# Reordering the attention part of the two "b1" phases: banks, weights, gates and convolution taps of a two-block network on one core

## The reference

```python
def hybrid_layer(x, ...):
    h = rmsnorm(x, norm_g)
    proj = h @ w_in                          # 1024 -> 3584
    y_a = conformer_conv(a_u, a_v, ...) * silu(a_z)   # 31-tap depthwise conv, layernorm, silu
    y_b = short_gated_conv(b_b, b_c, b_x, ...) * silu(b_z)
    y_c = window_gqa(c_q, c_k, c_v, sink) * silu(c_z)         # 4 query heads, 2 kv heads, rope
    y_d = neighborhood_attn(d_q, d_k, d_v, rpb) * silu(d_z)   # 4 heads, bias and mask
    return x + concatenate([y_a, y_b, y_c, y_d]) @ w_out
```

## Time and profile before

| | |
|---|---|
| median of three runs | 1233.93 us (1233.7 to 1235.58) |
| profiled execution | 1233.93 us, its span 1231.9 us |
| PE | busy 1222.0 us, 99% |
| DVE | busy 868.5 us, 71% |
| ACT | busy 682.1 us, 55% |
| POOL | busy 159.1 us, 13% |
| first b1 phase on PE | about 7 to 121 us |
| second b1 phase on PE | about 121 to 235 us |

### The profile page before, as it was taken

How to read it: one execution, slowest core, us unless ns; L and a number is a source line. 1 busy time by engine, 2 the same in 40 slices (tenths; PEclk the granted TensorE clock), 3 DMA queues, 4 the chain that set the end, 5 groups by cost and what they waited for, 6 DMA issues and landing times.

```text
span 1231.9 us, 24119 instructions
## 1 busy us (share of the span) xinstructions
PE 1222.0 (99%) x10072; PEld 1152.8 (94%) x10072; DVE 868.5 (71%) x1368; ACT 682.1 (55%) x1102; POOL 159.1 (13%) x210
## 2 busy tenths in 40 slices
PE   9999999999999999999999999999999999999997
PEld 7889888999999988899999999999998889999997
DVE  6998799877675567777676556667546777766742
ACT  7565665755554475565555445455447556555541
POOL 4102500473001200021000100000120003000001
PEclk9999999999999999999999999999999999999999
DMA  8545644556555554336555556555555434565551
GB/s 315 193 145 175 227 137 155 189 189 221 186 189 196 185 171 138 128 135 219 188 183 194 190 184 208 189 204 195 191 164 187 135 124 138 206 206 191 187 188 35
DMA packets 61387, 221.08 MB, mean 179 GB/s; under 512 B 7264, under 2 KB 7392, under 8 KB 61024
## 3 DMA queue, kind: packets, MB, share of 16 engines
q1 hardware_dynamic: 60768, 218.87, 53.2%
q0 software_dynamic: 224, 0.53, 0.2%
q10 hardware_dynamic: 288, 0.16, 0.0%
HBM read 218.48 MB, written 1.05 MB: 178 GB/s over the span
## 4 chain that ended last, share of the span: by engine, by line
PE 93%; DVE 3%; POOL 1%; DMA 1%; issue 1%; ACT 0%; SPq 0%; POOLq 0%; DVEq 0%; ACTq 0%
PE pb L486 13%; PE pb L484 13%; PE pb L485 13%; PE pb L499 8%; PE pb L501 8%; PE pb L500 8%; PE pb L464 7%; PE pb L466 7%; PE pb L465 7%; PE pb L559 3%; PE pb L588 1%; DVE s_acc L1367 1%; DVE s_wl L1225 1%; PE pb L616 1%; DMA s_wraw<-in_w 1%
## 5 line engine op out<-in xcount | busy, mean ns | idle before, releaser
L1225 DVE TENSOR_TENSOR s_wl<-s_wraw,s_wh 128x1024 fp32r<-128x1024 f32 (+1 forms) x411 | 503.9, 1247 | 120.0 <-ACT s_wh L868 119.6
L868 ACT ACTIVATE s_wh<-s_wraw 128x1024 fp32r<-128x1024 f32 (+1 forms) x411 | 420.4, 1049 | 183.2 <-PE pb L486 83.0
L484 PE MATMUL pb<-s_xh,s_wh 128*128 128x256 f32 x1296 | 359.1, 277 | 0.0
L486 PE MATMUL pb<-s_xh,s_wl 128*128 128x256 f32 x1296 | 358.3, 276 | 0.0
L485 PE MATMUL pb<-s_xl,s_wh 128*128 128x256 f32 x1296 | 358.3, 276 | 0.0
L485 PEld LDWEIGHTS pb<-s_xl,s_wh 128*128 128x128 f32 x1296 | 243.5, 188 | 0.0
L484 PEld LDWEIGHTS pb<-s_xh,s_wh 128*128 128x128 f32 x1296 | 243.5, 188 | 0.0
L486 PEld LDWEIGHTS pb<-s_xh,s_wl 128*128 128x128 f32 x1296 | 243.4, 188 | 0.0
L499 PE MATMUL pb<-s_hh,s_wh 128*128 128x256 f32 x660 | 182.2, 276 | 0.0
L500 PE MATMUL pb<-s_hl,s_wh 128*128 128x256 f32 x660 | 182.2, 276 | 0.0
L501 PE MATMUL pb<-s_hh,s_wl 128*128 128x256 f32 x660 | 182.2, 276 | 0.0
(11 more groups left out here) (316 smaller groups left out, 1566.8 us busy)
## 6 DMA issues: line engine op xcount, KB each, us to landing
s_wraw<-in_w SPq DMA_DIRECT2D x407, 512.0 KB, 4.0
s_nab<-in_rpb SPq DMA_DIRECT2D x2, 1024.0 KB, 8.9
s_x<-in_x SPq DMA_DIRECT2D x4, 256.0 KB, 6.0
out_dram<-s_at_s SPq DMA_DIRECT2D x4, 256.0 KB, 2.7
s_cst<-in_cst SPq DMA_DIRECT2D x1, 680.0 KB, 10.1
s_wraw<-in_w SPq DMA_DIRECT2D x2, 256.0 KB, 4.4
s_ln<-in_lng POOLq DMA_DIRECT2D x2, 128.0 KB, 7.3
s_ln<-in_lnb POOLq DMA_DIRECT2D x2, 128.0 KB, 7.9
```

The lines of the kernel that those rows point to most:

```text
L484: pe.matmul(o, wh[:, s, w], xk[0], start=k == v == 0, stop=False, skip_group_check=True)
L486: r = pe.matmul(o, wl[:, s, w], xk[0], start=False, stop=k == 7, skip_group_check=True)
L868: return act.activation(o, src, ACT.Copy, scale=scale)
L1225: dve.tensor_tensor(wl[:, s, part], wraw[:, r, part], wh[:, s, part].bitcast(F32), ALU.subtract).then_inc(low_done, 1)
```

## The change

It touches only the two b1 phases. On PE: the transposes of C's queries and keys come at tile 22 (first layer) or 23 (second), not at 26. The transposes of C's second half of weights come at tile 39, not 42. `weigh` for C and for the first half of D moves from tile 46 to tile 42, and only the second half of D stays at 46, where the transposes of the gates now follow it. The names `yC`, `yD`, `zC`, `zD` change places in the bank order. On ACT: silu of `az` is taken straight from PSUM between the exponentials of the two halves, where it was a copy there and a silu later; C's second exponentials come one unit later. On DVE: `low_c(1)` moves behind two weight units and four taps; `low_d(1)`, the products with the gates and the last taps move too, and two small steps of the lower bounds are in another place. `zc` has its own memory in place of that of `cr1`, and the turned weights of D's two halves share two slots, so ACT waits for `weighed_d0` before it copies the second.

```diff
@@ MISC["b1"], end of the tuple
-           ... "tC10", "tC11", "tD10", "tD11", "zC", "zD", "yC", "yD", "conv", "bx", "yA", "bz"),
+           ... "tC10", "tC11", "tD10", "tD11", "yC", "yD", "zC", "zD", "conv", "bx", "yA", "bz"),
@@ memory
+    zc = sb("zc", [P, 512], F32, arena)
-    zc = cr1[:, :, :].rearrange("p t c -> p (t c)")[:, 0:512]
-    at1 = Attention(arena, "at1", 8)
+    at1 = Attention(arena, "at1", 6)
@@ turned_slot
         if a == "D":
-            return 6 * t + kt
+            return kt
@@ PE, mixers1
-            tiles(n, 26)
+            tiles(n, 23 if l else 22)
             pe.wait_ge(rope_done, 2 * l + 2)
             turn_block(n, "cq", ...)
             turn_block(n, "ck", ...)
+            tiles(n, 26)
...
             tiles(n, 36)
             turn_weights(n, "D", 0)
             score_d(1)
+            tiles(n, 39)
+            turn_weights(n, "C", 1)
             tiles(n, 42)
-            turn_weights(n, "C", 1)
             turn_weights(n, "D", 1)
+            weigh(n, "C", value_c)
+            pe.wait_ge(dv_done, 2 * l + 2)
+            weigh(n, "D", value_d, (0,), (weighed_d0, 1))
             tiles(n, 46)
+            weigh(n, "D", value_d, (1,))
             for j, a in enumerate("CD"):
                 pe.wait_ge(gate_done[a], 2 * l + 2)
                 turn_block(n, "z" + a, ...)
-            weigh(n, "C", value_c)
-            pe.wait_ge(dv_done, 2 * l + 2)
-            weigh(n, "D", value_d)
@@ ACT, mixers1
+            split(n, 16)
+            act.wait_ge(*full(n, "cq"))
+            copy(flat(cqt[:, :, :]), psum(n, "cq")[:, :]).then_inc(*empty(n, "cq"))
             split(n, 17)
...
             turned_weights(n, "C", 0, 1, None)
-            exponential(n, "C", 1)
             for t in range(2):
                 act.wait_ge(main_done, projected(n, 3, t))
                 copy(dv[:, t, :], ...).then_inc(dv_done, 1)
-                copy(az[:, t, :], ..., r(t)).then_inc(*empty(n, ("in", 3, t)))
+            for t in range(2):
+                act.activation(az[:, t, :], psum(n, ("in", 3, t))[:, 256:512], ACT.Silu, scale=r(t)).then_inc(
+                    *empty(n, ("in", 3, t)))
             split(n, 22)
+            exponential(n, "C", 1)
+            split(n, 23)
             turned_weights(n, "D", 0, 0, None)
             turned_weights(n, "D", 0, 1, None)
+            split(n, 24)
             exponential(n, "D", 1)
+            turned_weights(n, "C", 1, 0, None)
+            turned_weights(n, "C", 1, 1, None)
             split(n, 25)
...
-            turned_weights(n, "C", 1, 0, None)
-            turned_weights(n, "C", 1, 1, None)
+            act.wait_ge(weighed_d0, l + 1)
             turned_weights(n, "D", 1, 0, None)
             turned_weights(n, "D", 1, 1, None)
-            act.activation(az[:, :, :], az[:, :, :], ACT.Silu).then_inc(az_done, 1)
@@ DVE, mixers1
             split(n, 19)
-            low_c(1, "tC01")
             conv(16 if l else 13)
             split(n, 20)
             conv(17 if l else 14)
...
             split(n, 21)
             conv(19 if l else 16)
+            low_c(1, "tC01")
+            split(n, 22)
+            conv(21 if l else 17)
+            split(n, 23)
             low_d(1, "tD01")
...
+            if l:
+                conv(25)
+                split(n, 25)
+                gated("C", 0)
+                gated("D", 1)
+                conv(28)
             split(n, 26)
             conv(29 if l else 26)
-            split(n, 27)
-            conv(31 if l else 27)
             product("C", zc)
             product("D", zd)
-            conv(31 if l else 28)
+            conv(30 if l else 27)
             product_low("C", zc, 4)
             product_low("D", zd, 6)
+            split(n, 27)
             conv(31 if l else 29)
```

More of the change, by code:

```diff
@@ L126 @@
     "b1": ("sum", "gate", "cq", "ck", "dq", "dk", "sC0a", "sC0b", "sD0a", "sD0b", "tC00", "tC01", "sC1a", "sC1b",
-           "tD00", "tD01", "sD1a", "sD1b", "tC10", "tC11", "tD10", "tD11", "zC", "zD", "yC", "yD", "conv", "bx", "yA", "bz"),
+           "tD00", "tD01", "sD1a", "sD1b", "tC10", "tC11", "tD10", "tD11", "yC", "yD", "zC", "zD", "conv", "bx", "yA", "bz"),
     "f": ("sum", "rbc"),
@@ L340, in program @@
     ya_done, cv_done, dv_done, rope_done = sem("ya_done"), sem("cv_done"), sem("dv_done"), sem("rope_done")
-    yh_done, az_done = sem("yh_done"), sem("az_done")
+    yh_done, weighed_d0 = sem("yh_done"), sem("weighed_d0")
     gate_done = {a: sem("gate_done" + a) for a in "CD"}
@@ L603, in turn_weights, with weigh @@
                     turn(o[:, P * h:P * (h + 1)], s[:, h, P * kt:P * (kt + 1)], fill(n, name) if h == 3 else None)
-        def weigh(n, a, value, ts=(0, 1)):
+        def weigh(n, a, value, ts=(0, 1), done=None):
             kts = [keys_of(a, t) // P for t in range(2)]
@@ L618, in weigh @@
                                           skip_group_check=True)
-            r.then_inc(*fill(n, "y" + a))
+            r.then_inc(*(done or fill(n, "y" + a)))
         def turn_block(n, name, src, count=2):
@@ L986, in mixers1 @@
             split(n, 18)
-            act.wait_ge(*full(n, "cq"))
-            copy(flat(cqt[:, :, :]), psum(n, "cq")[:, :]).then_inc(*empty(n, "cq"))
             act.wait_ge(*full(n, "dq"))
@@ L1002, in mixers1 @@
                 copy(dv[:, t, :], psum(n, ("in", 3, t))[:, 0:256], r(t)).then_inc(dv_done, 1)
-                copy(az[:, t, :], psum(n, ("in", 3, t))[:, 256:512], r(t)).then_inc(*empty(n, ("in", 3, t)))
+            for t in range(2):
+                act.activation(az[:, t, :], psum(n, ("in", 3, t))[:, 256:512], ACT.Silu, scale=r(t)).then_inc(
+                    *empty(n, ("in", 3, t)))
             split(n, 22)
+            exponential(n, "C", 1)
+            split(n, 23)
             turned_weights(n, "D", 0, 0, None)
             turned_weights(n, "D", 0, 1, None)
+            split(n, 24)
             exponential(n, "D", 1)
+            turned_weights(n, "C", 1, 0, None)
+            turned_weights(n, "C", 1, 1, None)
             split(n, 25)
@@ L1016, in mixers1 @@
                     *empty(n, ("in", 4, t)))
-            turned_weights(n, "C", 1, 0, None)
-            turned_weights(n, "C", 1, 1, None)
+            act.wait_ge(weighed_d0, l + 1)
             turned_weights(n, "D", 1, 0, None)
             turned_weights(n, "D", 1, 1, None)
-            for t in range(2):
-                act.wait_ge(*gone(n, ("in", 3, t)))
-            act.activation(az[:, :, :], az[:, :, :], ACT.Silu).then_inc(az_done, 1)
             split(n, 26)
@@ L1310, in lower_bounds_start @@
             lb = [pcols("lb", 4 * j, 4) for j in range(2)]
-            m, e0, e1 = (lbt[:, j, :] for j in range(3))
+            m, e0, e1, s = (lbt[:, j, :] for j in range(4))
             dve.wait_ge(ld_par, 16)
@@ L1316, in lower_bounds_start @@
             dve.tensor_tensor(e1, lb[1], m, ALU.subtract).then_inc(lb_step, 1)
+            dve.wait_ge(lb_exp, 2)
+            dve.tensor_tensor(s, e0, e1, ALU.add).then_inc(lb_step, 1)
+            dve.wait_ge(lb_step, 4)
+            dve.reciprocal(s, s).then_inc(lb_step, 1)
         def lower_bounds_end():
@@ L1321, in lower_bounds_end @@
             top = float(np.float32(1.0 - 1e-6))
[L1322 to L1325, removed]
             dve.wait_ge(lb_step, 5)
@@ L1459, in conv_gate @@
                 dve.wait_ge(act_a_done, l + 1)
-                dve.wait_ge(az_done, l + 1)
+                dve.wait_ge(*gone(n, ("in", 3, 0)))
+                dve.wait_ge(*gone(n, ("in", 3, 1)))
                 dve.tensor_tensor(an[:, :, :], an[:, :, :], az[:, :, :], ALU.mult).then_inc(ya_done, 1)
@@ L1505, in mixers1 @@
             conv(19 if l else 16)
+            low_c(1, "tC01")
+            split(n, 22)
+            conv(21 if l else 17)
+            split(n, 23)
             low_d(1, "tD01")
[L1507 to L1510, removed]
+            conv(22 if l else 19)
             reciprocals(n, "C", 1)
-            split(n, 23)
-            conv(22 if l else 19)
             split(n, 24)
@@ L1516, in mixers1 @@
             reciprocals(n, "D", 1)
[L1517 to L1520, removed]
+            if l:
[4 more added lines that the diff above has]
+                conv(28)
+            else:
+                lower_bounds_start()
+                conv(22)
+                split(n, 25)
+                gated("C", 0)
+                gated("D", 1)
                 lower_bounds_end()
-            split(n, 25)
-            conv(28 if l else 24)
-            if not l:
+                conv(24)
                 forget_weights()
+                conv(25)
             split(n, 26)
             conv(29 if l else 26)
-            split(n, 27)
-            conv(31 if l else 27)
             product("C", zc)
             product("D", zd)
-            conv(31 if l else 28)
+            conv(30 if l else 27)
             product_low("C", zc, 4)
             product_low("D", zd, 6)
+            split(n, 27)
```

## The result

The changed kernel takes 1243.69 us (median of 4 runs, 1243.14 to 1245.58), the kernel before 1234.76 us in the same comparison: a ratio of 1.0073 with a 95% interval of 1.0059 to 1.0085. It is slower, as forecast, but by more: 1239.8 us was forecast and the range ended at 1243.0. The profiled execution took 1242.35 us with a span of 1240.5 us; its mean granted clock is 0.996 of full speed, where that of the kernel before was 0.998. One more execution of the changed kernel (1356.44 us), and later one of six of e10 (1354.71 us), ran in a slow state at a mean clock of 0.85; they are left out of all figures. Two things have to be told apart: what PE newly waits for, and what its clock does after the waits.

A forecast was written before the change was run, and what follows sets the result against it. PE's order of work was taken as the bound (busy 1222.0 of 1231.9 us). First layer 2.35 + 0.2 - 0.4 = 2.15, second 2.37 + 0.2 + 1.2 = 3.77, together 5.9 on 1233.93: 1239.8 us, range 1236.5 to 1243.0.

The forecast's parts named there:

- The scores (2.35 and 2.37): PE waits at D's second scores for C's late reductions on DVE: +2.35 us first layer, +2.37 second.
- 1.71 + 0.05 + 0.80 = 2.56: From DVE's reductions to PE's next tile: 1.71 us until the fourth ends, 0.05 semaphore, 0.80 for remaining heads.
- the three heads left: PE's remaining heads of D's second scores before the next tile: 0.80 us, three quarters of 1.06.
- The ten tap instructions of the sum: On DVE, part of the nine rows now ahead of C's reductions; with two units and the reciprocals, 6.56 us.
- The clock: Sum: no cost. Rival: each of PE's two stops brings half speed, 2 us twice, 1243.8 us; chance 0.04.
- Taps (+1.2): Second layer's last taps stand behind the gates' products on DVE, so PE waits at the convolution's transposes: +1.2 us.
- ACT hidden, late by 0.7 without the stop: ACT's copies for PE's tile 39, with added table loads: hidden by 1.6 us; without the scores' stop, 0.7 late.
- Splits (+0.2): PE's 16 transposes split into two groups of eight, with the change of matmul kind: +0.2 us a layer.
- `an` (-0.4): PE's first-layer wait for the gated result `an` goes, as PE comes later than DVE's chain: -0.4 us.

The follow-up runs named there:

- e10: Kernel before with C's second reductions moved later on DVE in both layers, one tap fewer ahead of them than in e4: 1239.9 us, ratio 1.0047.
- e4: Kernel before with only C's second reductions moved to just ahead of D's on DVE, in both layers: 1241.87 us, ratio 1.0064.
- e5: Changed kernel with 14 unneeded matmuls of 256 columns filling PE's stop ahead of D's second scores, both layers: 1241.14 us, ratio 1.0057.
- e6: The changed kernel, unchanged, run once more on another chip, beside the kernel before: 1243.37 us, ratio 1.0071.
- e1: Changed kernel with C's second reductions put back at their old place on DVE in both layers: 1237.77 us, ratio 1.0032.
- e3: Changed kernel with C's second reductions and the second layer's last two taps both at their old places: 1236.48 us, ratio 1.0018.
- e8: Same as e3, with the silu of `az` also at its old place, so two table loads fewer per layer: 1234.59 us, ratio 1.0003.
- e9: Kernel before with C's second reductions moved as in e4, and two more taps ahead of them in each layer: 1246.94 us, ratio 1.0103.

## Why the prediction was wrong in its time and right in its stops

**The scores (2.35 and 2.37).** Right in place and cause, and small by a quarter of a microsecond. e4 isolates it: from the start of DVE's reductions (64.97 in its first layer) to the next tile of PE (67.79) are 2.82 us, where I had 1.71 + 0.05 + 0.80 = 2.56. The term that was too small is the 0.80 for "the three heads left": from the end of the fourth reduction (64.97 + 1.71 = 66.68) to the next tile are 1.11 us, not 0.85. The ten tap instructions of the sum are right; they are five taps, not the four that the section on the change names. In the first layer of e4 PE loses 2.57 us by it (67.79 for 65.88, though it was 0.66 early at the transposes). In the second layer of the changed kernel it is 3.03 us (6.88, less the 3.85 by which PE was late at the start of that layer's tiles, 139.53 for 135.68), also because DVE was already 0.4 us behind PE: its unit started at 178.66 for 174.41, 4.25 later. That 0.4 is DVE's sum of the rotated values, 1.29 us where it took 0.89 before, held up by POOL as shown at e5. I had no term for it. It was 1.75 us in e4 and 1.85 in e6, and from D's first scores to tile 36 of that layer PE lost 3.5 and 3.4 us there (5.66 and 5.98 us late at the tile, 2.15 and 2.55 at the scores), against 3.0 in the changed kernel's first profile.

**The clock.** This is the step that missed the range. The sum put a fall of the clock at nothing. I had it as a rival, at 1243.8 us, and gave it 0.04; that this time is so near to the 1243.69 measured is in part luck, for it has the waits 1.2 us too small (5.9 for 7.1) and the clock too large (4 us where about 2.2 were measured). I read the earlier trace rows as saying that the clock stays at 1.00 through a window half idle, and falls in one that is empty. The stop of a little over 2 us lay between these, and I took its side without a row that decided it. The same trace had one: PE's last matmuls start at 1225.57, after 1.04 us of idle time, and end at 1226.22, and the window from 1227 to 1228 us is already at 0.67. So there the clock fell after idle times that were each shorter than the stops that I forecast. What the runs showed in place of nothing: a fall behind a stop of 2.1 or 2.6 us takes 1.6 us by the rows, and about 2.2 us are gone from the usual run where filling keeps the clock up (e5). The range should have held two falls, some 3.3 us, on top of the sum, since no row spoke against them. "TensorE: Matmul & The Clock Gate" in the Trainium skill, section "Part 1: The HAM clock gate", ties the fall to idle time. The runs agree, and e4 adds that one and the same stop brings it in one execution and not in the next.

**Taps (+1.2).** Right: 1.38 us in the profile, 1.3 by e1 against e3. The product started at 210.12, 5.7 us later than before.

**ACT hidden, late by 0.7 without the stop.** Right on both counts: D's copies were forecast to end at 70.8 and end at 70.76 (69.71 + 1.05), with no wait in the changed kernel, and PE waits for them 1.6 us in two places once the stops are gone (e1, e3). So the two gains of undoing overlap: the stops alone had covered the table loads. The two added loads of the first layer are here, with the instruction behind each:

```profile
62.29 1.28 ACT L1007 ACT_TABLE_LOAD   x1
63.59 0.84 ACT L1007 ACTIVATE s_az<-pb,s_rs 128x256 f32<-128x256 f32 x2
...
65.39 1.28 ACT L939 ACT_TABLE_LOAD   x1
66.68 0.51 ACT L939 ACTIVATE s_at_s<-s_at_s,s_at_stat 128x256 f32<-128x256 f32 x1
```

1.30 and 1.29 us from start to start. The 2.66 us of "ScalarE: Activation LUTs" in the Trainium skill, section "What ACT_TABLE_LOAD costs", is not seen.

**Splits (+0.2), `an` (-0.4).** From tile 36 to tile 46 of the second layer PE lost 0.33 us (7.21 less 6.88) for the 0.2. The wait for `an` is gone where PE is late, and back with 0.3 us in e8, where it is not.

The sum as it measured: 2.57 + 3.03 (scores) + 1.4 (taps) + 0.5 (splits, 0.2 of it taken over for the first layer) - 0.4 + 2.2 (clock) = 9.3 us, for the 9.2 between 1243.37 and 1234.18. The terms come from different executions, so that they agree so closely is partly chance. Without the clock it is 7.1 for the 5.9 forecast, and 1234.18 + 7.1 = 1241.3 us would have been in the range.

## What to carry over

Where PE is full, a wait put on it costs its length, and here, at stops of 2 us and more, a fall of the clock on top of it in some of the executions. One profile shows only one draw. So look at the clock of all runs, not of the profiled one alone, and put such a case into the range with its whole price. A wait of PE for DVE is best taken away by giving PE other work there: two tiles ahead of the scores did as much as DVE's old order.

## What was not expected of the hardware

For one and the same kernel the fall comes in some executions only: with stops of 2.1 and 2.6 us one run had none and four had a mean clock of 0.995 or 0.993 (e4); with 1.3 to 1.6 us (e10) still four of five were at 0.996 or 0.997; with 3.7 and 4.2 us (e9) all were at 0.995 or less. The kernel before, without such stops, was at 0.997 to 0.999 in all runs beside the experiments. It need not come in the stop: in the first layer of the changed kernel PE starts again at 66.58, and the clock falls only in the window from 67 on; in e9, where PE starts again at 68.16, it falls in the same window, with PE still idle. And its size is nearly always the same: the clock column lacks 1.70 or 1.71 us in four of the five falls in the layers and ahead of them, and twice that in the fifth.

A DVE instruction of 0.56 us can take up to 2.63 us beside POOL: the sum of the rotated values ends 2.81 to 2.86 us after the start of POOL's work on `nab` in all twelve traces, whenever it starts itself.
